# Retention states of the sample tokens read before they are decayed, and three smaller moves around it

## The chip, the cores and the metric

The kernel runs on one core of one Trainium2 chip. The time is the device time of one execution in microseconds (us), the median of several. A core has a matrix engine (TensorE, PE; PEld is its load of the stationary operand), a vector engine (VectorE, DVE), ScalarE (ACT), GpSimd (POOL), SyncE (SP, which here only issues transfers), and 16 DMA engines that move data between its on-chip memory and HBM.

## What is computed

One layer of a decoder for two groups that share the weights: 256 prompt tokens and 8 sample tokens (264 columns in all), width 1024, float32. What the change touches:

```
mkv = rmsnorm(mem_prompt, norm_mem) @ w_mem_kv          # memory keys and values, 256 rows
mk, mv = jnp.split(mkv, 2, axis=-1)                      # both are also outputs
# retention, per head (4 heads, DK = 256, DV = 512); for a sample token the chunk is one token long
att = einsum('bhnk,bhmk->bhnm', qc, kc) * dmask
o = einsum('bhnm,bhmv->bhnv', att, vc) + einsum('bhnk,bhkv->bhnv', qc * q_decay[..., None], s)
s = s * s_decay + einsum('bhmk,bhmv->bhkv', kc * k_decay[..., None], vc)
o = o * lax.rsqrt(mean(o * o, axis=-1) + EPS)
```

For a sample token the query meets the state as it comes in: o = (q.k) v + gamma (q @ s), and the state that goes out is gamma s + k v. That is equal to q @ (gamma s + k v). Behind the mixers, which are projected and merged, comes a mixture of 32 experts whose weights (192 MB) are streamed once.

## The kernel before

Activations lie transposed, 8 tiles of 128 channels by 264 tokens. `tensor_order` (L274) writes out one list of tasks for the whole kernel up to the router, and PE, ACT and DVE each walk that list and do their part of a task, in order, with semaphores between them. A projection task (`ux`, `q`, `ga`, `lru_out`, ...) gives one tile of 128 output channels: 8 float32 products of 128x128 by 264 columns (`project`, L940), which the profile counts as 16 matmul records. Two tasks share a weight chunk of 1 MB. SP loads chunks into a ring of five; chunk n is issued once the last task on chunk n-5 is done on PE. Results go to PSUM, four banks in turn for projections and three for the rest (bank 7 is apart), and ACT or DVE empties a bank before its next use. `weave(main, side)` spreads one list evenly over another.

**Start.** SP issues the memory rows `memT` in two halves, the constants, chunk 0, `xT` and the next chunks. ACT squares the memory rows, PE sums the squares over channels with 8 products by a matrix of ones (`column_sums`, L959), ACT takes the root, DVE the reciprocal and then norms eight tiles (L1548); `mk` (L990) starts on these. `mk` gives keys as rows (token by channel), and four `mkT` tasks (L1013, 4 transposes each) turn them. The squares of `x` go the same way (`x_sq`, 8 products).

**States.** There are 16 sample states of 1 MB, each two heads of one sample (task number s), in three buffers `st`. POOL issues the load (L853) and, after the update, the store (L878). The row of v that a state needs is first moved to partition 0 (L859) and then spread over the partitions (L863, `partition_broadcast`). Task `sd` decays a state in place on ACT (L1268, 2 instructions) and adds k v on DVE (L1701, 4 instructions); task `so` on PE (L1136) multiplies the updated state by the query of its sample, into bank 7, at row group 32h for head h. In POOL's loop, each turn is: wait for the update of s, store s, move the row for s+2 and wait for it, broadcast, load s+2. The `sd` of the next state stands ahead of `so` in the list, on ACT and DVE too. Around them run the 32 projections `ga`, `lru_out`, `gc`, `mem_out`, and the prompt's retention: `att` (scores of a head, L1111 and L1114, masked by DVE into the one buffer `attT`, L1691) and four `o` per head (L1124).

**After the states.** `soT` turns the samples' result (L1144, 4 transposes), then per head ACT squares (`oq`), PE sums (`on`, 4 products, L959) and DVE norms. `gb`, `g`, `ret_out` and `x2` projections follow, then the router. SP issues the first expert weights when `ret_ready` has counted all 16 tiles of the gated retention (after the last `g`); from some 750 us on the experts run behind the stream of weights (L770).

## Time and profile before

| | us |
|---|---|
| median of 3 runs (1208.28 to 1210.97) | 1209.36 |
| the profiled execution, its own time | 1210.15 |
| its span | 1208.3 |
| PE busy | 988.2 (82%) |
| DVE busy | 361.3 (30%) |
| ACT busy | 225.6 (19%) |
| POOL busy | 99.4 (8%) |
| DMA, mean over the span | 285 GB/s |

The profile is of one execution. Busy time is by engine; what counts is who waits for whom in each stretch. The stretches are: memory keys and values up to about 77 us, projections and gates to 317 us, the states to about 510 us, the rest of the mixers to 700 us, the router to 766 us, the experts to 1192 us.

### The profile page before, as it was taken

How to read it: one execution, taken by the hardware profiler on the slowest of the kernel's cores; microseconds unless marked ns; L12 is line 12 of the kernel's file. 1: busy time of each engine (PE TensorE's matmuls, PEld its weight loads, DVE VectorE, ACT ScalarE, POOL GpSimd, SP SyncE). 2: the span in 40 equal slices, each digit the busy share in tenths (PEclk: the TensorE clock that was granted, in tenths of full speed). 3: DMA queues.
4: the chain of work that ended last, by engine and by line, in shares of the span. 5: the costliest groups of instructions: out<-in, count | busy, mean ns of one | idle time of the engine just before them, and what ended most of it. 6: DMA issues, size and time to landing. Idle time of an engine off the chain costs nothing.

```text
span 1208.3 us, 16378 instructions
## 1 busy us (share of the span) xinstructions
PE 988.2 (82%) x7006; PEld 716.5 (59%) x7006; DVE 361.3 (30%) x660; ACT 225.6 (19%) x465; POOL 99.4 (8%) x122
## 2 busy tenths in 40 slices
PE   6999999999998899799999978666666665665654
PEld 5888888778775566488888835433333333333323
DVE  1201583376223334323211172111135111111113
ACT  2211213204412221142100051101010101010102
POOL 0001111000123233100000050000000000000000
PEclk9999999999999899899999999999987889899888
DMA  9764557494667787643534958999999999999991
GB/s 289 242 233 161 175 178 274 162 294 114 216 224 248 272 290 248 236 139 120 194 106 139 383 208 339 417 417 416 417 416 416 416 416 417 417 417 417 417 411 69
DMA packets 138826, 343.80 MB, mean 285 GB/s; under 512 B 7640, under 2 KB 91864, under 8 KB 122360
## 3 DMA queue, kind: packets, MB, share of 16 engines
q1 hardware_dynamic: 124288, 290.04, 63.7%
q0 software_dynamic: 14464, 52.68, 12.3%
q8 instruction: 58, 0.95, 0.3%
q14 instruction: 16, 0.13, 0.0%
HBM read 320.46 MB, written 22.20 MB: 284 GB/s over the span
## 4 chain that ended last, share of the span: by engine, by line
PE 46%; SPq 24%; DMA 11%; issue 7%; DVE 7%; ACT 3%; POOL 2%; DVEq 0%; ACTq 0%; POOLq 0%
PE psum L940 27%; SPq L770 24%; DMA arena<-in_w_up 6%; PE psum L990 5%; DMA arena<-in_state_ret 4%; PE psum L949 2%; PE psum L682 2%; ACT arena L1268 2%; DVE arena L1701 2%; DMA arena<-arena 1%; PE psum L692 1%; PE psum L959 1%; POOL arena L863 1%; PE psum L666 1%; DVE arena L1600 1%
## 5 line engine op out<-in xcount | busy, mean ns | idle before, releaser
L940 PE MATMUL psum<-arena 128*128 128x264 f32 x2048 | 473.1, 388 | 0.0
L940 PEld LDWEIGHTS psum<-arena 128*128 128x128 f32 x2048 | 386.3, 190 | 83.9 <-issue 20.0
L682 PE MATMUL psum<-arena 128*32 128x256 f32 x2048 | 148.1, 440 | 119.4 <-DMA arena<-in_w_up 118.7
L682 PEld LDWEIGHTS psum<-arena 128*32 128x32 f32 x2048 | 79.0, 123 | 183.1 <-issue 160.5
L1268 ACT ACTIVATE arena<-psum 128x264 f32<-128x264 f32 (+4 forms) x180 | 75.1, 434 | 322.8 <-PE psum L940 251.9
L1268 ACT ACTIVATE arena<-arena 128x1024 f32<-128x1024 f32 (+7 forms) x67 | 58.7, 903 | 202.6 <-DMA arena<-in_state_ret 106.6
L1701 DVE SCALAR_TENSOR_TENSOR arena<-arena 128x512 f32<-128x512 f32 x64 | 52.9, 888 | 121.7 <-ACT arena L1268 107.1
L1887 DVE SCALAR_TENSOR_TENSOR arena<-arena,psum 128x128 f32<-128x128 f32 x32 | 9.2, 288 | 238.4 <-ACT arena L1476 238.4
L692 PE MATMUL psum<-arena 128*32 128x256 f32 x1024 | 65.2, 397 | 11.7 <-ACT arena L1488 11.7
L1196 PE MATMUL psum<-arena 128*128 128x264 f32 x112 | 39.8, 438 | 25.9 <-DVE arena L1899 25.9
L990 PE MATMUL psum<-arena 128*128 128x256 f32 x256 | 56.3, 379 | 3.1 <-DVE arena L1548 3.1
L692 PEld LDWEIGHTS psum<-arena 128*32 128x32 f32 x1024 | 31.0, 113 | 39.7 <-ACT arena L1488 21.6
L990 PEld LDWEIGHTS psum<-arena 128*128 128x128 f32 x256 | 48.2, 190 | 9.8 <-issue 3.4
L1476 ACT ACTIVATE arena<-psum 128x128 f32<-128x128 f32 x32 | 8.9, 278 | 241.2 <-PE psum L682 241.2
L1136 PE MATMUL psum<-arena 128*8 128x512 f32 x128 | 36.4, 698 | 20.6 <-DVE arena L1701 20.6
L666 PEld LDWEIGHTS psum<-arena 128*128 128x128 bf16 x576 | 35.4, 104 | 16.9 <-issue 16.9
L666 PE MATMUL psum<-arena 128*128 128x128 bf16 x576 | 40.5, 230 | 1.6 <-DVE arena L1835 1.6
L1196 PEld LDWEIGHTS psum<-arena 128*128 128x128 f32 x112 | 17.2, 194 | 39.9 <-DVE arena L1899 37.5
L1842 DVE COPY arena<-psum 32x256 f32<-32x256 f32 x32 | 13.5, 421 | 75.7 <-PE psum L692 75.7
L1899 DVE TENSOR_TENSOR arena<-arena,psum 128x264 f32<-128x264 f32 x56 | 24.0, 428 | 38.7 <-PE psum L1196 38.7
L863 POOL PARTITION_BROADCAST arena<-arena x16 | 22.2, 1389 | 117.9 <-DMA arena<-arena 117.9
L949 PE MATMUL psum<-arena 128*128 128x264 f32 x128 | 29.8, 386 | 0.0
(236 smaller groups left out, 696.3 us busy)
## 6 DMA issues: line engine op xcount, KB each, us to landing
arena<-in_w_gate SPq DMA_DIRECT2D x64, 1024.0 KB, 23.0
arena<-in_w_up SPq DMA_DIRECT2D x64, 1024.0 KB, 22.5
arena<-in_w_down SPq DMA_DIRECT2D x64, 1024.0 KB, 22.9
arena<-in_w_in SPq DMA_DIRECT2D x48, 1024.0 KB, 5.2
arena<-in_state_ret POOLq DMA_DIRECT2D x16, 1024.0 KB, 6.5
out_ret_s<-arena POOLq DMA_DIRECT2D x16, 1024.0 KB, 7.9
arena<-in_w_mem_kv SPq DMA_DIRECT2D x8, 1024.0 KB, 9.6
arena<-in_cache_mem_k POOLq DMA_DIRECT2D x8, 1024.0 KB, 5.7
```

Source lines behind the costliest of these rows:

```text
L666: mm = pe.matmul(psum[:, 5 + k // 4, (k % 4) * P:(k % 4 + 1) * P], xr[x][:, t, k * P:(k + 1) * P], Sb[:, t, :], start=t == 0 and x == 0, s ...
L682: mm = pe.matmul(psum[32 * a:32 * a + SLOTS, bank, 0:256], tokens[:, 4 * half + k, SLOTS * j:SLOTS * (j + 1)], w[:, :, k, P * a:P * (a + 1 ...
L692: mm = pe.matmul(psum[32 * a:32 * a + SLOTS, bank, 0:256], hidden[:, SLOTS * (2 * half + f):SLOTS * (2 * half + f + 1)], w[:, f, 256 * a:2 ...
L770: sp.dma_start(into(s, i), expert_part(e, i)).then_inc(chunk_loaded[s], 16)
L863: nc.gpsimd.partition_broadcast(vb[:, s % 2, :], v_row0[0:1, :], P).then_inc(v_bcast, 1)
L940: mm = pe.matmul(ps(task)[:, 0:T], w[:, k, (i % 2) * P:(i % 2 + 1) * P], rhs[:, k, :], start=k == 0, stop=k == KT - 1 and not two)
L949: mm = pe.matmul(ps(task)[:, 0:T], w[:, k, (i % 2) * P:(i % 2 + 1) * P], rhs[:, KT + k, :], start=False, stop=k == KT - 1)
L990: mm = pe.matmul(ps(task)[:, 0:256], memT[:, k, m * P:(m + 1) * P], w[:, k, :], start=k == 0, stop=k == KT - 1)
L1136: mm = pe.matmul(psum[32 * h:32 * h + NS, 7, :], QM[:, 2 * h + i, b, :], st[:, s % 3, 2 * h2 + i, :], start=b == 0 and i == 0, stop=b == N ...
L1196: pe.matmul(psum[:, 7, 0:T], yS[:, (q - 1) % 2, d * P:(d + 1) * P], SwT[:, (q - 1) % 2, :], start=True, stop=True).then_inc(scatter_full, 1)
L1268: steps.did(nc.scalar.activation(out, in_, func, **kw), sem)
L1701: did(V.scalar_tensor_tensor(x, vb[:, s % 2, h2 * DV:(h2 + 1) * DV], kT[:, 2 * (2 * hp + h2) + i, TP + b:TP + b + 1], x, ALU.mult, ALU.add ...
```

## The change

1. **Start.** `chan` (channel constants) is issued first, chunk 0 between the halves of `memT`. DVE scales the memory rows by `norm_mem` alone (`memS`), and `mk` and `mv` run on these. The factor of a row (one over its root mean square) is applied as results leave PSUM: for `mk`, which is now computed already transposed (weights stationary), by DVE; for `mv` by ACT, with a column that the new task `mrow` makes. `mkT` is gone. The output `mem_k` is stored from the transposed tile.
2. **Squares.** DVE adds the tiles of squares pairwise (`add_squares`), and `column_sums` is one product. It holds for `mem_sq`, `x_sq` and the four `on`.
3. **States.** `so` waits for the load of its state, not for the update, and stands ahead of `sd`; ACT's decay waits for `so`. Its four products go to four column groups (one per tile of the state, 16 columns each) instead of two. `soT` multiplies by a table `place`, which adds the two halves of a head and applies gamma; (q.k) v is made apart (tasks `qk`, and four DVE products at `vs`). The row of v is moved two states ahead into one of two buffers, and the load of s+2 is issued before the store of s.
4. **Scores.** `att` of the next head stands a head ahead, `attT` has two buffers.

The diff, cut to its core:

```diff
@@ tensor_order
-    ret = []
+    ret = [("att", 0)]
     for h in heads:
-        ret += [("att", h)] + [("o", h, j) for j in range(4)]
-    so = [("sd", 0)]
-    for s in range(2 * NS):
-        so += ([("sd", s + 1)] if s + 1 < 2 * NS else []) + [("so", s)]
+        ret += ([("att", h + 1)] if h + 1 < HEADS else []) + [("o", h, j) for j in range(4)]
+    so = [x for s in range(2 * NS) for x in (("so", s), ("sd", s))]
+    middle = weave(branches, ret[1:])
...
-        [("mem_sq",)] + t("mk", 8)[:2] + [("xq",)] + t("mk", 8)[2:4] + [("x_sq",), ("lam",)] + t("mk", 8)[4:]
-        + weave(t("mv", 8), t("mkT", 4)) + t("mq", 8) + t("mqs", 2)
+        t("mk", 8)[:2] + [("mem_sq",), ("xq",)] + t("mk", 8)[2:4] + [("mrow",)] + t("mk", 8)[4:6]
+        + [("x_sq",), ("lam",)] + t("mk", 8)[6:] + t("mv", 8) + t("mq", 8) + t("mqs", 2)
...
-        + weave(weave(branches, ret[1:]), so)
+        + middle[:4] + weave(middle[4:], so)
@@ gpsimd
+            def v_row(s):
+                b, hp = n_state(s)
+                if s >= 2:
+                    pool.wait_ge(v_bcast, s - 1)
+                pool.dma_start(v_row0[:, s % 2, :], vs_rows[b:b + 1, hp * D:(hp + 1) * D]).then_inc(v_row_in[s % 2], 16)
             def v_broadcast(s):
-                b, hp = n_state(s)
-                if s >= 1:
-                    pool.wait_ge(v_bcast, s)
-                pool.dma_start(v_row0[0:1, :], vs_rows[b:b + 1, hp * D:(hp + 1) * D]).then_inc(v_row_in, 16)
-                pool.wait_ge(v_row_in, 16 * (s + 1))
+                pool.wait_ge(v_row_in[s % 2], 16 * (s // 2 + 1))
                 if s >= 2:
                     pool.wait_ge(st_updated, s - 1)
...
+                if s + 2 < 2 * NS:
+                    v_row(s + 2)
...
             for s in range(2 * NS):
+                if s >= 1 and s + 2 < 2 * NS:
+                    load_state(s + 2)
                 pool.wait_ge(st_updated, s + 1)
                 pool.dma_start(dst, st[:, s % 3]).then_inc(st_out[s % 3], 16)
                 if s + 2 < 2 * NS:
                     v_broadcast(s + 2)
-                    if s >= 1:
-                        load_state(s + 2)
@@ tensor
+            def column_sums(task, src, cols, n):
+                pe.wait_ge(squares_added, n)
+                begin(task)
+                end(task, pe.matmul(ps(task)[:, 0:cols], ones, src[:, 0, 0:cols], start=True, stop=True))
...
+                        mm = pe.matmul(ps(task)[:, 0:TP], w[:, k, (i % 2) * P:(i % 2 + 1) * P], memS[:, k, :],
+                                       start=k == 0, stop=k == KT - 1)
...
                 elif kind == "so":
-                    pe.wait_ge(st_updated, s + 1)
-                    for i in range(2):
-                        for h2 in range(2):
-                            h = 2 * hp + h2
-                            mm = pe.matmul(psum[32 * h:32 * h + NS, 7, :], QM[:, 2 * h + i, b, :],
-                                           st[:, s % 3, 2 * h2 + i, :],
-                                           start=b == 0 and i == 0, stop=b == NS - 1 and i == 1)
+                    pe.wait_ge(q_placed, 2)
+                    pe.wait_ge(st_in[s % 3], 16 * (s // 3 + 1))
+                    for g in range(4):
+                        mm = pe.matmul(psum[32 * g:32 * g + 2 * NS, 7, :], QM[:, 4 * hp + g, b, :], st[:, s % 3, g, :],
+                                       start=s == 0, stop=s == 2 * NS - 1)
                     mm.then_inc(st_read, 1)
@@ scalar
                     act.wait_ge(st_in[s % 3], 16 * (s // 3 + 1))
+                    act.wait_ge(st_read, s + 1)
@@ vector
+            for q in range(2):
+                dve.wait_ge(mem_in[q], 16)
+                did(V.tensor_tensor(memS[:, 4 * q:4 * q + 4, :], memT[:, 4 * q:4 * q + 4, :],
+                                    bc(cvs("norm_mem")[:, 4 * q:4 * q + 4].unsqueeze(2), (P, 4, TP)), ALU.mult), mem_scaled)
...
+            def take_mem_keys(i):
+                full(dve, ("mk", i))
+                v(V.tensor_tensor(mkT[:, i, :], ps(("mk", i))[:, 0:TP], rstd[:, 0, 0:TP], ALU.mult), free_of(("mk", i)))
```

The order of PE's instructions at the start, before. L959 is the sum of squares, L990 `mk` and then `mv`, L1013 `mkT`:

```order
L959 MATMUL psum<-arena 128x256 x8
L990 MATMUL psum<-arena 128x256 x32
L959 MATMUL psum<-arena 128x264 x8
L990 MATMUL psum<-arena 128x256 x40
L1013 MATMUL psum<-arena 128x128 x4
```

And now, where L1015 is `mk`, L1027 `mv`, L978 a sum of squares, L1002 `mrow`:

```order
L1015 MATMUL psum<-arena 128x256 x16
L978 MATMUL psum<-arena 128x256
L1015 MATMUL psum<-arena 128x256 x16
L1002 MATMUL psum<-arena 128x8 x2
L1015 MATMUL psum<-arena 128x256 x16
L978 MATMUL psum<-arena 128x264
L1015 MATMUL psum<-arena 128x256 x16
L1027 MATMUL psum<-arena 128x256 x64
```

Two tasks of `mk` stand ahead of the first sum, each sum is one product, and no transposes stand between the projections.

POOL's queue in the loop over the states, before, with what each waits for. L859 moves the row of v, L863 (ISA) broadcasts it, L853 loads a state, L878 stores one:

```order
L859 DMA arena<-arena 1x16x64 [waits v_bcast]
L863 ISA arena<-arena 128x1024 [waits st_updated,v_row_in]
L853 DMA arena<-in_state_ret 128x4x512 [waits st_read,st_out_0]
L878 DMA out_ret_s<-arena 128x4x512 [waits st_updated]
L859 DMA arena<-arena 1x16x64 [waits v_bcast]
```

And now, with L873 for the row, L880 for the broadcast, L866 for the load and L901 for the store:

```order
L880 ISA arena<-arena 128x1024 [waits st_updated,v_row_in_0]
L873 DMA arena<-arena 1x16x64 [waits v_bcast]
L866 DMA arena<-in_state_ret 128x4x512 [waits st_read,st_out_0]
L901 DMA out_ret_s<-arena 128x4x512 [waits st_updated]
L880 ISA arena<-arena 128x1024 [waits st_updated,v_row_in_1]
```

The row is now issued behind the broadcast, for a state two further on; the load is held only by the store of the state that had its buffer, and no broadcast stands between that store's landing and the load.

PE at the start of the states, before. L940 is a projection, L1111 and L1114 `att`, L1124 and L1125 `o`, L1136 `so`:

```order
L1111 MATMUL psum<-arena 128x256 x2
L1114 MATMUL psum<-arena 128x128 x2
L940 MATMUL psum<-arena 128x264 x8
L1124 MATMUL psum<-arena 128x256
L1125 MATMUL psum<-arena 128x128
L940 MATMUL psum<-arena 128x264 x8
L1124 MATMUL psum<-arena 128x256
L1125 MATMUL psum<-arena 128x128
L1136 MATMUL psum<-arena 8x512 x4
```

And now, L961 a projection, L1139 and L1142 `att`, L1152 and L1153 `o`, L1164 `so`:

```order
L1139 MATMUL psum<-arena 128x256 x2
L1142 MATMUL psum<-arena 128x128 x2
L961 MATMUL psum<-arena 128x264 x8
L1139 MATMUL psum<-arena 128x256 x2
L1142 MATMUL psum<-arena 128x128 x2
L961 MATMUL psum<-arena 128x264 x8
L1152 MATMUL psum<-arena 128x256
L1153 MATMUL psum<-arena 128x128
L961 MATMUL psum<-arena 128x264 x8
L1164 MATMUL psum<-arena 16x512 x4
```

The second `att` comes before the first `o`, and the first `so` one projection later; the number of products of `so` is the same, with 16 stationary columns instead of 8.

## Rows read from the trace of the kernel before

**Rows 1.** Busy time by stretch: PE, weight loads, DVE, ACT, POOL, granted clock, DMA

```profile
core 0: us, PE busy (x) PEld busy (x) DVE busy (x) ACT busy (x) POOL busy (x), PEclk, DMA share, GB/s
...
168.00:317.00 149.00, 148.74 (x778) 120.32 (x777) 79.81 (x58) 41.23 (x84) 15.83 (x20) 1.00 0.64 205
345.00:510.00 165.00, 145.04 (x623) 98.83 (x621) 55.72 (x78) 34.15 (x51) 43.38 (x52) 0.95 0.77 264
...
766.00:1192.00 426.00, 265.13 (x3274) 149.52 (x3262) 88.58 (x230) 48.33 (x132) 0.00 (x0) 0.90 0.99 405
```

**Rows 2.** PE in order of time, first 60 us: start, duration, instructions

```profile
7.29 5.71 PE L959 MATMUL psum<-arena 128*128 128x256 f32 x16 [7.29 <-ACT arena L1268]
...
16.07 14.05 PE L990 MATMUL psum<-arena 128*128 128x256 f32 x64 [3.07 <-DVE arena L1548]
...
29.96 3.72 PE L959 MATMUL psum<-arena 128*128 128x264 f32 x16
...
50.79 0.60 PE L1013 MATMUL psum<-arena 128*128 128x128 f32 x4
```

**Rows 3.** DMA issues at 0.7, 2.8 and 4.4 us: KB each, us to landing

```profile
arena<-in_memT SPq DMA_DIRECT2D x1, 512.0 KB, 4.0
...
arena<-in_w_mem_kv SPq DMA_DIRECT2D x1, 1024.0 KB, 7.4
...
arena<-in_w_mem_kv SPq DMA_DIRECT2D x1, 1024.0 KB, 11.8
```

**Rows 4.** Who waited for whom, 317 to 515 us: total, times, longest

```profile
POOL arena L863 <- DMA arena<-arena: 117.9, 16, 10.4
...
PE psum L1136 <- DVE arena L1701: 20.6, 6, 5.9
...
PE psum L1124 <- DVE arena L1691: 2.4, 2, 1.6
```

**Rows 5.** PE in order of time, state stretch; in brackets idle time before

```profile
320.37 1.10 PE L1111 MATMUL psum<-arena 128*128 128x256 f32 x4
...
352.95 1.89 PE L1136 MATMUL psum<-arena 128*8 128x512 f32 x8
...
366.78 3.36 PE L1136 MATMUL psum<-arena 128*8 128x512 f32 x8 [3.31 <-DVE arena L1701]
...
506.63 3.41 PE L1136 MATMUL psum<-arena 128*8 128x512 f32 x8 [2.40 <-DVE arena L1701]
```

**Rows 6.** The chain of waits in the same stretch: start, duration

```profile
372.83 2.01 ACT arena L1268 x2
...
375.63 3.01 DVE arena L1701 x3
```

**Rows 7.** DMA queues (packets, MB, share) and issues, 317 to 515 us

```profile
q0 software_dynamic: 9216, 33.62, 48.1%
q1 hardware_dynamic: 16153, 16.28, 25.4%
...
arena<-in_state_ret POOLq DMA_DIRECT2D x16, 1024.0 KB, 6.5
out_ret_s<-arena POOLq DMA_DIRECT2D x16, 1024.0 KB, 7.9
```

**Rows 8.** The stores of the states, line L878, all sixteen

```profile
DMA to landing us min/median/max: 4.7/7.9/11.4
```

**Rows 9.** Line L878 from 350 to 370 us: stores right behind a load

```profile
L878 POOL DMA_DIRECT2D out_ret_s<-arena x2: 759/773/787, 353.3 to 367.0; - x2
...
DMA to landing us min/median/max: 8.3/9.8/11.2
```

**Rows 10.** The chain of waits in the expert stage, one line

```profile
748.95 3.45 PE psum L682 x64
```

**Rows 11.** PE in order of time, behind the states: one `on`

```profile
524.76 1.94 PE L959 MATMUL psum<-arena 128*128 128x264 f32 x8
```

**Rows 12.** SyncE's issues: the first load of an expert's weights

```profile
664.32 0.46 SPq L755 DMA_DIRECT2D arena<-in_w_gate  x1
```

More of the change, by code:

```diff
@@ L121 @@
     "memT": (KT * TP, "load", "mem"),
+    "memS": (KT * TP, "load", "mem"),
+    "mrow": (8, "load", "mem"),
     "sq": (KT * T, "load", "mem"),
@@ L951, in project @@
                 end(task, mm)
-            def column_sums(task, src, n, cols, first=None):
+            def column_sums(task, src, cols, n):
+                pe.wait_ge(squares_added, n)
                 begin(task)
-                for k in range(n):
-                    if first is not None and k % 4 == 0:
-                        pe.wait_ge(squares, first + k // 4)
-                    mm = pe.matmul(ps(task)[:, 0:cols], ones, src[:, k, 0:cols], start=k == 0, stop=k == n - 1)
-                end(task, mm)
+                end(task, pe.matmul(ps(task)[:, 0:cols], ones, src[:, 0, 0:cols], start=True, stop=True))
             def residual_squares(k):
@@ L1023, in _ @@
                     _, h, l = task
-                    read(pe, ("mkT", 3))
+                    read(pe, last["mk"])
                     read(pe, last["mq"])
```

184 lines of the change are left out of this document (119 added, 65 removed).

## The prediction

> **What bounds the kernel now.** I read busy time by stretch first. From 168 to 317 us PE is busy 148.7 of 149 us: a microsecond of PE work less there is a microsecond off the time. From 766 to 1192 us the DMA share is 0.99, and no engine sets the pace: the stream of expert weights takes its length whenever it starts [rows 1]. SyncE issues its first load at 664.3 us [rows 12], behind the last `g` on PE. So the end moves with PE's arrival there, and the question is how much earlier PE arrives. The stretch ahead of it in which PE is not full is 345 to 510 us, with 145.0 of 165 us busy at a granted clock of 0.95 [rows 1].
>
> Next, who waits there: PE for DVE's state update ahead of `so`, 20.6 us in six waits, and 2.4 us for the masked scores [rows 4]. Behind them POOL waits 117.9 us, sixteen times, for the one row of v, because that 4 KB transfer is queued behind a 1 MB store and often a load, and the next load is issued only after it. After some waits `so` also runs slower: 3.36 us behind an idle 3.31 us, 1.89 us at 352.95 with no wait [rows 5], which is the lower of the two clock levels (1.2 GHz) against the higher (2.4 GHz). A wait so costs a little more than itself.
>
> **Start.** PE's first `mk` begins at 16.1 us, after squares summed from 7.3 us, root, reciprocal and norm [rows 2]. Now it needs only DVE's scaled rows and chunk 0. The first chunk landed at 2.8 + 7.4 = 10.2 us, the second at 4.4 + 11.8 = 16.2 us [rows 3], with `xT` (1056 KB) and itself between: 6.0 us for 2 MB, 3.0 us per MB. Some 0.7 MB that stood ahead of chunk 0 now stand behind it, so it lands at about 8.0 us and the second half of `memT` at 9.5. DVE's scaling of a half I put at 1.2 us (four tiles; the first `mk` waits for the second half at 10.7 us). `mk` 0 ends at about 13 and `mk` 1 at 16.5 us, where two took (16.07, 14.05 for four) until 23.1: 6.6 us gained. Chunk 1 lands at 16.2, just in time. Each sum of squares shrinks from 16 records (3.72 us, [rows 2]) to 2, say 0.45: for `x_sq` 3.2 us gained; the memory's own, formerly under the start, now costs 0.45, and `mrow` 0.5. The four `mkT` (0.60 us of records each, [rows 2], some 0.43 in the flow) give 1.7 us. DVE's pairwise adds (1.8 records of a 1056-column pass, about 2 us) and evacuations lie beside `mk` work; if DVE were late the fifth `mk` would wait for its bank, but it has 6 us. Sum 6.6 + 3.2 + 1.7 - 1.0 = 10.5; I take **10**, from 7 (chunk 1 late by 3 us) to 11.
>
> The small task `qk` adds two products, 0.5 us.
>
> **States, PE's own work.** The stretch from the first `att` (320.4) to the first `gb` (510.0 + 3.6 = 513.6: `so` 15 ends at 510.0 [rows 5], and `mem_out` 7 follows) is 193.2 us. Take away the waits, 23.0 us [rows 4], and the slow clock behind four of them (1.5 us each, 3.36 against 1.89 [rows 5]) and one slow projection, 7 us. What is left is 163. `so` costs 1.89 us for 8 records of 512 columns in two column groups. Over four groups the expert stage gives the price: 64 records of 256 columns in 3.45 us [rows 10], 0.054 each, so 8 of twice the columns 0.86 us, with a switch 0.95. Sixteen times 0.94 less is 15: PE's floor for the stretch is **148**, with `so` 15 at 143 and one `so` each 8.9 us.
>
> **States, the other chain.** Once PE no longer waits for the update, a buffer comes free only when its store has landed, and POOL waits for exactly that ahead of the next load. A turn of its loop is then: wake 0.3, issue a load 0.8, issue the store, its landing L. So the period is P = L + 1.1 us, and PE waits for it wherever P is above 8.9. The first `so` comes about 14.3 us after `att` (two `att`, three projections, one `o`); then 0.95, decay 2.0, update 3.7 (four instructions; three take 3.0) [rows 6], and gaps give the first store at 22. The load for state 15 is issued 13 P - 0.8 later and lands 6.5 us after [rows 7]: `so` 15 starts at 27.6 + 13 P. What is L? All sixteen stores land in 4.7, median 7.9, at most 11.4 us [rows 8]. But the changed loop issues each store right behind a load; two such cases took 8.3 and 11.2 [rows 9], and the 11.4 is another: mean 10.3. I take the middle of 7.9 and 10.3, **9.1**, since the row's wait, which made POOL late and the pairs tight, is gone. P is 10.2, `so` 15 at 160.2, and `gb` 0 5.3 us later (`so`, one `o`, one projection) at 165.5 instead of 193.2: **27.7** gained. The waits of some 1.3 us each are shorter than those behind which the clock had fallen. DMA agrees that it is close: 33.6 MB of states took 48.1% of 198 us, 3.0 us per MB, and 16.3 MB of weights 25.4%, 3.2 us per chunk [rows 7]; a period moves two and one, 9.2 us of 16 engines.
>
> The masked scores a head ahead take the 2.4 us, already in. The row of v, two ahead, hides behind a period.
>
> **A page on this.** The Trainium skill (DMA: Bandwidth & Descriptors, Queues, rings and completion order) says that each DMA engine takes turns between the queues that have work, packet by packet. This speaks against the change: a pair of load and store shares with a weight chunk whenever SP has one. By that rule the tight pairs' 11.2 and 8.3 us are one with a chunk beside it and one without, and with a chunk each time the sum would be that of the slow loop below, 1183 or more. The same page (Anatomy of one DMA) fits a transfer as 2.0 us plus bytes at 436 GB/s, by which I estimate 4.4 us for a state; with that the loop would never hold PE, and the sum would be 1151 us. The fastest store here took 4.7 us and the median 7.9, so the trace decides for the longer.
>
> **Behind the states.** Four `on` of 8 records (1.94 us, less 0.16 of overlap, [rows 11]) become 2 records each: 5.3 us gained. `soT` goes from 4 transposes to 8 short records with full weight loads, 0.8 us lost. DVE's two adds per head and ACT's first square, which waits for the last store (now some 11 us after `so` 15, as the update comes behind it), lie under `gb` tasks of 3.6 us. Sum **4.5**.
>
> **Sum.** 10 - 0.5 + 27.7 + 4.5 = 41.7. Against the profiled execution (1210.15) that is 1168.5; it stands 0.8 above the median of the runs, so 1167.7. I say **1168 us**.
>
> **Rivals.**
> - *PE's floor.* Stores land in 7.8 us or less, the loop hides, and `gb` 0 comes at 148.7: 44.5 in place of 27.7, 1151 us. For it: the median landing of 7.9 (P 9.0), and no broadcast between. Against: DMA has 9.2 us of work in 8.9. Chance 0.30.
> - *The loop is slow.* Load, store and chunk share all the way: L of 10.3 gives P 11.4, `so` 15 at 175.8, 15.6 us worse: 1183. At L 11.4 (the longest) 1198. For it: the tight pairs. Chance 0.20, some 0.05 of it above 1192.
> - *The change does not free PE.* `so` reads a raw state, yet the wait just changes its name from update to load, at the old pace. `so` 15 would come 186 us after the first `att`, as now (506.6 - 320.4 [rows 5]), and only the 14 us of start, `qk` and end are gained, with 1.7 of a shorter tail: 1193.5. That is a period of 12.2, and its chance is in the 0.05 just named.
> - *Slower.* The mechanism is the same loop, in order on POOL: a late store holds the next load, and with it the store behind it. The total is 1209.35 - 14 - (193.2 - 32.9 - 13 P), which crosses 1209.3 at P = 13.4, a store landing of 12.3 us. At P = 14 it gives 1217. Speaking for it: DMA would be asked for more in less time than before. Against: no store of the sixteen took over 11.4 [rows 8]. Chance 0.05.
> - Within 0.2%: only by chance between the last two, 0.02.
>
> **How the numbers follow.** The forecast, P between 9.6 and 10.9 and so 1160 to 1177 us, has 0.43. Low 1148 is PE's floor with 3 us more from the start; high 1192 leaves out the end of the slow loop, no gain and slower, about 0.12, and below 1148 I leave 0.04. A measurement of this kernel tells 0.2% (2.4 us) from no change. Faster by more 0.93, within 0.02, slower 0.05.
>
> **What would show it.** `mk` begins near 9 us with a short wait for the second half, and `x_sq` is one product. `so` takes 0.95 us. PE's waits for a DVE update are gone and waits of 1 to 3 us for the state's DMA stand in their place, in the later half, some 15 us in all; stores land in about 9 us. From the first `gb` to the first expert load everything is as before but 4.5 us shorter, and the expert stretch keeps its 426 us. The forecast is wrong if `so` waits for nothing (first rival), if stores take over 10 us, or if the start shows a wait for chunk 1.

## The result, and the profile of the changed kernel

The changed kernel takes 1172.63 us (median of four runs, 1167.83 to 1174.22), the kernel before 1208.82 (median of four, 1201.39 to 1210.97). The ratio is 0.9705, with a 95% interval of 0.9654 to 0.9755. The forecast was 1168, with a range of 1148 to 1192. The profiled execution took 1173.44 us with a span of 1171.6 us, where that of before had 1208.3: 36.7 us less. Three places in the trace divide this sum into four parts, and each has its forecast:

| part of the span | before | after | gained | forecast |
|---|---|---|---|---|
| to the first `att` | 320.4 | 311.15 | 9.2 | 9.5 |
| first `att` to first `gb` | 193.2 | 172.0 | 21.2 | 27.7 |
| first `gb` to the first expert load | 150.7 | 145.8 | 4.9 | 4.5 |
| first expert load to the end | 544.0 | 542.7 | 1.3 | 0 |

The start first: four separate lines from PE's and DVE's order of time, 0 to 75 us. The bracket gives the idle time just before and what ended it.

```profile
8.63 8.80 PE L1015 MATMUL psum<-arena 128*128 128x256 f32 x32 [8.63 <-DMA arena<-in_w_mem_kv]
...
10.06 1.23 DVE L1578 TENSOR_TENSOR arena<-arena 128x1024 f32<-128x1024 f32 x1 [3.51 <-DMA arena<-in_memT]
...
17.26 0.59 PE L978 MATMUL psum<-arena 128*128 128x256 f32 x2
...
31.96 0.61 PE L978 MATMUL psum<-arena 128*128 128x264 f32 x2
```

PE begins `mk` at 8.63 us where it began at 16.07 [rows 2]. Chunk 0 is what it waited for, and it came 0.6 us behind the time of the working (8.0 us). The scaling of the second half takes 1.23 us, as taken, and both sums are two records instead of sixteen. The two tasks end at 17.4 us, a microsecond later than worked out. No wait for chunk 1 follows: the one wait of PE up to 80 us is that of 8.6 us for chunk 0.

Next the stretch that mattered: busy time by stretch, with the columns of [rows 1], first the stretch of the states, then the expert stage.

```profile
311.00:483.00 172.00, 154.43 (x739) 116.77 (x737) 55.48 (x88) 44.01 (x68) 50.52 (x59) 0.97 0.85 281
...
729.00:1155.00 426.00, 268.15 (x3286) 150.52 (x3278) 88.91 (x232) 48.09 (x132) 0.00 (x0) 0.90 0.99 405
```

PE is busy 154 of 172 us, so it is still not the bound there. The expert stage is 426 us at a share of 0.99, as before [rows 1]. Who waited for whom, 300 to 495 us (total, times, longest), the view of [rows 4]:

```profile
POOL arena L866 <- DMA out_ret_s<-arena: 82.4, 13, 8.5
...
POOL out_ret_s L901 <- DVE arena L1772: 25.2, 3, 11.6
...
PE psum L1164 <- DMA arena<-in_state_ret: 17.4, 11, 3.0
...
POOL arena L880 <- DMA arena<-arena: 8.3, 1, 8.3
```

Read it from the top. POOL's 117.9 us of waits for the row of v [rows 4] have shrunk to one of 8.3 us, and in their place POOL waits 82.4 us, thirteen times, for a store to land before it may issue a load (L866). PE's 20.6 us of waits for DVE's update are gone, and 17.4 us of waits for a state's load stand there: in all, PE waits only 5.6 us less than before (17.4 against 23.0). One turn of POOL's loop and the start of the next, in order of time, show its period:

```profile
405.20 0.79 POOL L866 DMA_DIRECT2D arena<-in_state_ret  x1 [5.60 <-DMA out_ret_s<-arena]
405.98 0.76 POOL L901 DMA_DIRECT2D out_ret_s<-arena  x1
406.76 1.29 POOL L880 PARTITION_BROADCAST arena<-arena  x1
...
415.48 0.78 POOL L866 DMA_DIRECT2D arena<-in_state_ret  x1 [6.61 <-DMA out_ret_s<-arena]
416.26 0.76 POOL L901 DMA_DIRECT2D out_ret_s<-arena  x1
```

Load and store are issued 0.8 us apart, and the next load comes as soon as that store has landed: 10.28 us from L866 to L866. The thirteen loads of the loop (340.61 to 467.83 us) are 10.6 us apart in the mean. The landings in this stretch, the view of [rows 7], with the median in the last column:

```profile
arena<-in_state_ret POOLq DMA_DIRECT2D x16, 1024.0 KB, 7.1
out_ret_s<-arena POOLq DMA_DIRECT2D x16, 1024.0 KB, 9.3
```

Last, PE in order of time, as [rows 5] shows it for before:

```profile
325.27 1.05 PE L1164 MATMUL psum<-arena 128*16 128x512 f32 x8
...
369.37 1.05 PE L1164 MATMUL psum<-arena 128*16 128x512 f32 x8 [1.95 <-DMA arena<-in_state_ret]
370.35 1.22 PE L1152 MATMUL psum<-arena 128*128 128x256 f32 x2
...
392.89 1.05 PE L1164 MATMUL psum<-arena 128*16 128x512 f32 x8 [3.03 <-DMA arena<-in_state_ret]
...
394.96 5.07 PE L961 MATMUL psum<-arena 128*128 128x264 f32 x16
...
476.19 1.91 PE L1164 MATMUL psum<-arena 128*16 128x512 f32 x8 [2.61 <-DMA arena<-in_state_ret]
...
479.47 7.36 PE L961 MATMUL psum<-arena 128*128 128x264 f32 x32
```

`so` takes 1.05 us in four column groups, where it took 1.89 in two [rows 5]. The last `so` begins 165.0 us after the first `att` (476.19 - 311.15); before it was 186.3, and the forecast 160.2.

### The profile page after: what moved, and what is told of

It is laid out like the page before. It is cut to its first block, busy times and chain, and to the rows that moved or that the text cites. A ratio compares the mean times of both kernels' runs of the same rounds, so it can differ in the third digit from the quotient of the medians.

```text
span 1171.6 us, 16329 instructions
## 1 busy us (share of the span) xinstructions
PE 961.7 (82%) x6950; PEld 705.9 (60%) x6950; DVE 366.6 (31%) x681; ACT 221.4 (19%) x453; POOL 100.9 (9%) x122
## 4 chain that ended last, share of the span: by engine, by line
PE 47%; SPq 22%; DMA 20%; DVE 5%; issue 4%; ACT 2%; POOL 1%; DVEq 0%; ACTq 0%; POOLq 0%
PE psum L961 28%; SPq L783 22%; DMA out_ret_s<-arena 10%; DMA arena<-in_w_up 8%; PE psum L693 3%; PE psum L1015 3%; PE psum L970 2%; PE psum L1027 2%; PE psum L703 2%; PE psum L677 1%; ACT arena L1301 1%; DVE arena L1664 1%; DMA arena<-arena 1%; POOL arena L866 1%; DMA arena<-in_state_ret 1%
## 5 line engine op out<-in xcount | busy, mean ns | idle before, releaser
L961 PE MATMUL psum<-arena 128*128 128x264 f32 x2048 | 473.6, 388 | 0.0
L961 PEld LDWEIGHTS psum<-arena 128*128 128x128 f32 x2048 | 387.6, 191 | 76.3 <-issue 12.0
L1301 ACT ACTIVATE arena<-psum 128x264 f32<-128x264 f32 (+5 forms) x160 | 67.5, 439 | 350.8 <-PE psum L961 269.0
L703 PE MATMUL psum<-arena 128*32 128x256 f32 x1024 | 66.4, 402 | 11.8 <-ACT arena L1522 11.7
L1772 DVE SCALAR_TENSOR_TENSOR arena<-arena 128x512 f32<-128x512 f32 x64 | 45.6, 774 | 82.0 <-ACT arena L1301 81.9
L1229 PEld LDWEIGHTS psum<-arena 128*128 128x128 f32 x112 | 17.1, 193 | 38.6 <-DVE arena L1977 36.1
L1015 PE MATMUL psum<-arena 128*128 128x256 f32 x128 | 30.1, 396 | 8.6 <-DMA arena<-in_w_mem_kv 8.6
L1301 ACT ACTIVATE arena<-psum,arena 128x256 f32<-128x256 f32 (+2 forms) x49 | 22.8, 473 | 72.1 <-PE psum L1027 24.9
L1977 DVE TENSOR_TENSOR arena<-arena,psum 128x264 f32<-128x264 f32 x56 | 24.0, 428 | 36.7 <-PE psum L1229 36.7
L1015 PEld LDWEIGHTS psum<-arena 128*128 128x128 f32 x128 | 25.4, 200 | 12.3 <-issue 8.6
L1164 PE MATMUL psum<-arena 128*16 128x512 f32 x128 | 17.7, 624 | 17.6 <-DMA arena<-in_state_ret 17.4
```

Of the source, the lines that this page charges most:

```text
L703: mm = pe.matmul(psum[32 * a:32 * a + SLOTS, bank, 0:256], hidden[:, SLOTS * (2 * half + f):SLOTS * (2 * half + f + 1)], w[:, f, 256 * a:2 ...
L961: mm = pe.matmul(ps(task)[:, 0:T], w[:, k, (i % 2) * P:(i % 2 + 1) * P], rhs[:, k, :], start=k == 0, stop=k == KT - 1 and not two)
L1015: mm = pe.matmul(ps(task)[:, 0:TP], w[:, k, (i % 2) * P:(i % 2 + 1) * P], memS[:, k, :], start=k == 0, stop=k == KT - 1)
L1229: pe.matmul(psum[:, 7, 0:T], yS[:, (q - 1) % 2, d * P:(d + 1) * P], SwT[:, (q - 1) % 2, :], start=True, stop=True).then_inc(scatter_full, 1)
L1301: steps.did(nc.scalar.activation(out, in_, func, **kw), sem)
L1772: did(V.scalar_tensor_tensor(x, vb[:, s % 2, h2 * DV:(h2 + 1) * DV], kT[:, 2 * (2 * hp + h2) + i, TP + b:TP + b + 1], x, ALU.mult, ALU.add ...
```

## The experiments

Two theories stood against each other. **A** is the prediction's: with the wait for the update gone, POOL's loop (a load waits for the store before it) sets the pace, P = L + 1.1. **B** is its rival: the DMA engines are simply full (share 0.85 in this stretch), and the order on POOL matters little. The part-by-part experiments are made on the changed kernel, one on the kernel before. "Stretch" is first `att` to first `gb` in the run's own profile, of one execution each. Times of one kernel differ between executions: the four of the changed kernel span 6.4 us, four of another kernel below 9.9 us. Where only one execution was timed, a difference of a few microseconds is not told from none.

### Store ahead of the load

```diff
-                if s >= 1 and s + 2 < 2 * NS:
-                    load_state(s + 2)
                 pool.wait_ge(st_updated, s + 1)
                 pool.dma_start(dst, st[:, s % 3]).then_inc(st_out[s % 3], 16)
                 if s + 2 < 2 * NS:
                     v_broadcast(s + 2)
+                    if s >= 1:
+                        load_state(s + 2)
```

> The changed kernel with one move: POOL issues the store of state s and the broadcast ahead of the load of s+2, not behind it. The stretch from the first att to the first gb was 193.2 us before the change and 172.0 us with it, against a floor of PE work of 148. Theory A (POOL's order): a store that is ready stands behind a load that waits for the previous store to land, so the period is a landing plus 1.1 us; freed of that, the period falls to 8.9 to 9.3 us and the stretch to 150 to 157 us, the time to about 1155 us. Theory B (the DMA engines are simply full, share 0.85 in this stretch): the period stays at 10.3 to 10.6 us, the stretch at 168 to 172 us and the time at 1169 to 1173 us.

Measured: 1179.2 us (1175.2 to 1180.5) against 1206.3 for the kernel before on the same chip, ratio 0.9783 (0.975 to 0.9815); stretch 172.8. Theory A asked for a stretch of 150 to 157 us and missed. The stretch is just above B's 168 to 172, but the rows show another cause than B's. POOL in order of time, two stores and the load between, then its and PE's waits, 311 to 484 us:

```profile
411.05 0.75 POOL L899 DMA_DIRECT2D out_ret_s<-arena  x1 [9.35 <-DVE arena L1772]
...
413.95 0.79 POOL L866 DMA_DIRECT2D arena<-in_state_ret  x1
...
421.12 0.75 POOL L899 DMA_DIRECT2D out_ret_s<-arena  x1 [6.39 <-DVE arena L1772]
```

```profile
POOL out_ret_s L899 <- DVE arena L1772: 97.2, 14, 11.5
...
PE psum L1164 <- DMA arena<-in_state_ret: 18.8, 9, 5.4
```

No store is waited for by POOL any more (the sixteen land in a median of 5.8 us here). POOL now waits 97.2 us for DVE's *update*, and the load stands behind it in POOL's queue. The update in turn can start only behind `so`, which reads the raw state and needs its load. Four rows show that chain between the load at 413.95 and the load of s + 4 at 433.45:

```profile
420.29 1.05 PE L1164 MATMUL psum<-arena 128*16 128x512 f32 x8 [0.43 <-DMA arena<-in_state_ret]
...
425.13 0.39 ACT L1301 ACTIVATE arena<-psum 128x264 f32<-128x264 f32 x1 [4.86 <-PE psum L961]
425.42 1.99 ACT L1301 ACTIVATE arena<-arena 128x1024 f32<-128x1024 f32 x2
...
427.51 2.74 DVE L1772 SCALAR_TENSOR_TENSOR arena<-arena 128x512 f32<-128x512 f32 x4 [6.69 <-ACT arena L1301]
```

The load lands 6.2 us after its issue, `so` of s + 2 takes 1 us, the decay starts 4.1 us behind it, decay and update take 4.8, and 3 us later the load of s + 4 is issued: 19.5 us for two periods. The 4.1 us are no work on the state. `weave` has put a projection between `so` and `sd`, and ACT, in order, empties that projection's bank first (the row at 425.13). So POOL's queue in order, the raw read and this place in ACT's list hold the loop together. No run moves the decay right behind `so`.

### Reading the raw state with the old loop

```diff
+                v_row(s)
                 pool.wait_ge(v_row_in[s % 2], 16 * (s // 2 + 1))
...
-                if s + 2 < 2 * NS:
-                    v_row(s + 2)
```

(and the load behind the broadcast, as above, and no rows moved ahead of the loop)

> The changed kernel with POOL's loop as it was before: the row of v for s+2 is moved behind the store of s and waited for, then broadcast, then the load. so still reads the raw state. If the row's wait was what made the loop slow, the stretch from the first att to the first gb returns to 183 to 193 us (time 1184 to 1194). If the raw read is what frees PE, it stays near 172 us (time near 1173).

Measured: 1218.66 us, one execution; stretch 217.1, beyond the 183 to 193 expected for the row's wait, the last `so` 209.5 us after the first `att`. That is slower than the kernel before (1206.3 on this chip), in spite of the start, `on` and the column groups. Of the waits, 320 to 545 us:

```profile
POOL arena L881 <- DMA arena<-arena: 95.5, 16, 9.2
...
PE psum L1161 <- DMA arena<-in_state_ret: 54.8, 8, 10.5
```

POOL waits again sixteen times for the 4 KB row behind a big store, and PE pays 54.8 us. In the kernel before, the decay ran ahead of PE's `so` and hid part of that; a raw read puts `so`, decay and update in series behind each load. That reading is argued; what is shown is that with POOL's old loop the raw read, and the smaller moves beside it, come with a stretch 24 us longer than before. So the raw read does not make the gain.

### The decayed and updated state read, in the changed loop

```diff
-    so = [x for s in range(2 * NS) for x in (("so", s), ("sd", s))]
+    so = [("sd", 0)]
+    for s in range(2 * NS):
+        so += ([("sd", s + 1)] if s + 1 < 2 * NS else []) + [("so", s)]
...
-                    pe.wait_ge(st_in[s % 3], 16 * (s // 3 + 1))
+                    pe.wait_ge(st_updated, s + 1)
...
-                    act.wait_ge(st_read, s + 1)
```

> The changed kernel with so behind the update again, as before the change (the order of sd and so too), and the new POOL loop kept; the samples' result then counts the decay and k v twice, the work is the same. Theory A (POOL's loop with its store landings sets the pace): the period stays at 10.5 us and each so comes one decay and update later, 5 to 7 us, so the stretch is 177 to 181 us and the time about 1180. Theory C (the raw read is the gain): the stretch returns to 188 to 193 us, the time to 1189 to 1194.

Measured: 1178.83 us, one execution; stretch 177.8, the last `so` 170.4 us after the first `att`, 5 us later than in the changed kernel. Both are A's numbers (177 to 181, about 1180): the pace is the loop's, whichever form of the state PE reads. The raw read is worth some 6 us with this loop.

### A quarter of each store

```diff
-                pool.dma_start(dst, st[:, s % 3]).then_inc(st_out[s % 3], 16)
+                pool.dma_start(dst[:, 0:1], st[:, s % 3, 0:1]).then_inc(st_out[s % 3], 16)
```

> The changed kernel, but only a quarter of each state is stored (the rest of the output is left out), so a store moves 256 KB. If the waits of so for its load (17.4 us in eleven) come from stores that land late, the landing falls to 5 us or less, the waits go and the stretch is PE's floor of 148 to 151 us, the time 1149 to 1153. If something else holds PE there (evacuation by ACT or DVE, the decay and update), the stretch stays above 160 us.

Measured: 1157.05 us, one execution; stretch 152.9, the last `so` 147.6 us after the first `att`. The stores' landings and PE's waits, 311 to 530 us:

```profile
out_ret_s<-arena POOLq DMA_DIRECT2D x16, 256.0 KB, 5.4
...
PE psum L1164 <- DMA arena<-in_state_ret: 4.1, 2, 3.0
```

With stores landing in 5.4 us PE waits twice, and the stretch is 5 us above the floor of 148 that the prediction worked out. Stretch, time and landing are each a little above what was expected (148 to 151, 1149 to 1153, 5 or less). Both halves of A stand all the same: L holds the loop, and PE's own work below it is 148.8 (152.9 less 4.1 of waits). It does not tell whether what counts is the landing time or the bytes; the last experiments do.

### The store issued by ACT

```diff
+            def store_state(s):
+                b, hp = n_state(s)
+                act.wait_ge(st_updated, s + 1)
+                act.dma_start(dst, st[:, s % 3]).then_inc(st_out[s % 3], 16)
...
+                    if s >= 1:
+                        store_state(s - 1)
                     act.wait_ge(st_in[s % 3], 16 * (s // 3 + 1))
```

(and POOL stores nothing; ACT stores the last state at `soT`)

> The changed kernel with the stores of the states issued by ACT, each ahead of the next state's decay, and no store in POOL's queue. POOL then issues the load of s+2 when the store of s-1 has landed and nothing else waits behind it. Both POOL orders tried so far gave a period of 10.3 to 10.6 us: with the load first a ready store waits for a landing (82 us of such waits), with the store first a load waits for the update (97 us). Theory A (the coupling of loads and stores in one queue that is issued in order): the period falls to 8.9 to 9.4 us, the stretch from the first att to the first gb from 172 to 149 to 158 us, and the time to 1152 to 1161 us. Theory B (the DMA engines' throughput holds it at 10.3 us): 168 to 173 us and a time near 1172. Theory C (ACT becomes the bound, since it now waits for updates and empties banks late): 173 to 185 us.

Measured: 1185.96 us (1183.41 to 1189.73) against 1207.4, ratio 0.9862 (0.9785 to 0.9938); stretch 183.2. A had asked for a gain and failed here; 183.2 is in the range of theory C (173 to 185), in which ACT becomes the bound. The waits, 311 to 500 us:

```profile
POOL arena L866 <- DMA out_ret_s<-arena: 101.1, 12, 14.6
...
PE psum L1161 <- DMA arena<-in_state_ret: 26.6, 7, 7.2
```

ACT reaches the store only ahead of the next decay, and that is a period behind the update. The store lands faster (7.9 us) but starts later, and POOL waits 14.6 us for it at worst. C had named late emptying of banks by ACT as well; PE has no wait for it here. The second queue gained nothing, since the engine that feeds it comes by too seldom.

### Two column groups, scores behind, squares and the sum in their old places

Four kernels, one execution each, that undo one edit of the change. Two column groups in `so`:

```diff
-                    for g in range(4):
-                        mm = pe.matmul(psum[32 * g:32 * g + 2 * NS, 7, :], ...)
+                    for g in (0, 2, 1, 3):
+                        at = 32 * (g // 2)
+                        mm = pe.matmul(psum[at:at + 2 * NS, 7, :], ...)
```

(and `place` adds the two halves accordingly)

> The changed kernel with so's four products in two column groups, as before the change. Each so takes 1.85 to 1.9 us instead of 1.05. If the loop over the loads sets the pace from the fifth state on, most of it lies under the waits (17.4 us in eleven): the stretch grows from 172 by 2 to 5 us and the time to about 1176. If PE's work sets it, by 13 to 14 us, to 1186.

Measured: 1171.36 us, stretch 169.7, `so` 1.90 us. Sixteen times 0.85 us more on PE, and nothing lost, where 2 to 5 us were expected: it disappears in PE's waits for the loads, which are 7.1 us here instead of 17.4.

The scores of a head right ahead of its `o`:

```diff
-    ret = [("att", 0)]
+    ret = []
     for h in heads:
-        ret += ([("att", h + 1)] if h + 1 < HEADS else []) + [("o", h, j) for j in range(4)]
+        ret += [("att", h)] + [("o", h, j) for j in range(4)]
```

(and one buffer for `attT`)

> The changed kernel with each att directly ahead of its own head's o, and one buffer for the masked scores, as before the change. Before, PE waited 2.4 us in two places for it. If the loop over the states swallows it, the time stays within 3 us of 1172.6; otherwise it grows by 2 to 5 us.

Measured: 1173.96 us, stretch 171.0. No difference that one execution can tell.

All squares summed by PE, without DVE's adds:

```diff
-                end(task, pe.matmul(ps(task)[:, 0:cols], ones, src[:, 0, 0:cols], start=True, stop=True))
+                for k in range(tiles_):
+                    mm = pe.matmul(ps(task)[:, 0:cols], ones, src[:, k, 0:cols], start=k == 0, stop=k == tiles_ - 1)
+                end(task, mm)
```

> The changed kernel with the squares summed by PE as before (8 products for the memory and for x, 4 for each of four heads), nothing added on DVE. By the prediction's prices: 3.1 us for each of the first two and 5.3 for the four, 11.5 us, so about 1184. If PE's work is hidden in these places, less.

Measured: 1181.12 us. The first `att` comes at 317.6 instead of 311.15, 6.45 us later, and the part behind the states is 5.3 us longer; the stretch between is 166.5, 5.5 us shorter. So undoing the edit costs 8.5 us of the total (1184 was expected). In the two parts where PE is full it costs 11.8, and the loop gives some of that back.

The memory's sum ahead of the first `mk`, as before:

```diff
-        t("mk", 8)[:2] + [("mem_sq",), ("xq",)] + t("mk", 8)[2:4] + ...
+        [("mem_sq",)] + t("mk", 8)[:2] + [("xq",)] + t("mk", 8)[2:4] + ...
```

(and DVE's scaling behind the reciprocal)

> The changed kernel with the sum of the memory's squares ahead of mk again, and the scaled rows made only after its root and reciprocal (result the same). It takes out the early start alone. By the prediction PE's first mk comes near 17 to 18 us instead of 8.6 with a hold to 11, so the time grows by 6 to 8 us, to about 1180. If chunk 1 or a later chunk held mk anyway, it grows by less than 4.

Measured: 1182.18 us; the first `att` at 321.7, 10.6 us later, where 6 to 8 was expected. PE in order of time:

```profile
13.67 1.19 PE L978 MATMUL psum<-arena 128*128 128x256 f32 x2 [13.67 <-DVE arena L1581]
...
18.64 16.69 PE L1015 MATMUL psum<-arena 128*128 128x256 f32 x64 [3.77 <-DVE arena L1598]
```

DVE's adds end only at 13.67 us, later than PE's own sum over raw squares would (it began at 7.29 [rows 2]). Pre-added squares need the memory product ahead of them; put first, they leave PE idle for longer.

### The updated state read, and the store first

The first three experiments leave two couplings: with the raw read the update is late, with the load first the store must land. So I took both away: PE reads the updated state (and no `qk` product), and POOL issues the store, then the load. The result is whole. It is the two diffs above together, with the decay factor 1.0 in the placement table and the correction for `qk` left out:

```diff
-                place[32 * (2 * (h % 2) + i) + NS * (h // 2) + b, NS * h + b] = 1.0 - 2.0 ** (-5.0 - h)
+                place[32 * (2 * (h % 2) + i) + NS * (h // 2) + b, NS * h + b] = 1.0
```

> The changed kernel with so reading the updated state again (place holds 1 instead of gamma, and qk and its products are gone, so the result is whole), and with the store and the broadcast ahead of the load in POOL's queue. Everything else of the change stays. Theory A (a cycle of waits through the update): with the raw read the update starts only behind so, and with the store first the next load is issued behind that update, 10.3 us per state. Here decay and update start as the load lands: from one update to the load of s+2 3.2 us, its landing 6.8, decay 2.0 and update 3.7, 16 us for two states, so a period of 8 and PE's 8.9 decides. The stretch from the first att to the first gb falls from 172 to 149 to 156 us, the time to 1149 to 1158. Theory B (the DMA engines' throughput is the bound at 10.3 us however the waits lie): 168 to 175 us, the time 1169 to 1176.

Measured: **1152.39 us** (1151.96 to 1152.99) against 1206.3, ratio 0.956 (0.9528 to 0.9592); stretch 150.5. Its interval lies wholly below that of the changed kernel's ratio (0.9654 to 0.9755), so it beats both kernels. PE in order of time, then busy time of 155 us and of the middle of them, and PE's only waits for a state (two):

```profile
331.30 1.05 PE L1166 MATMUL psum<-arena 128*16 128x512 f32 x8 [1.13 <-DVE arena L1766]
...
340.25 1.05 PE L1166 MATMUL psum<-arena 128*16 128x512 f32 x8
...
349.20 1.05 PE L1166 MATMUL psum<-arena 128*16 128x512 f32 x8
```

```profile
325.00:480.00 155.00, 153.13 (x757) 117.28 (x756) 61.76 (x98) 50.03 (x72) 46.71 (x55) 1.00 0.88 309
...
340.00:450.00 110.00, 110.00 (x549) 82.85 (x548) 43.39 (x71) 33.89 (x50) 38.93 (x46) 1.00 0.99 347
```

```profile
PE psum L1166 <- DVE arena L1766: 1.9, 2, 1.1
```

One `so` each 8.95 us, PE busy 153.1 of 155 us with a granted clock of 1.00 throughout. The same states and weight chunks pass in less time than in the changed kernel: 309 GB/s at a share of 0.88 here, 281 at 0.85 there. Bytes and DMA engines were not what held that kernel, so B falls. But they are near their end in this one: from 340 to 450 us the share is 0.99, beside a PE that is busy throughout, and loads now land in a median of 9.3 us, stores in 7.5. The loop's period, for which 8 us had been counted with a landing of 6.8, is by this some 8.6 (by my estimate 3.2 + 9.3 + 2.0 + 2.7 us for two states), little less than PE's 8.95. How much a kernel with less PE work would still gain is not shown.

The same with two column groups in `so`:

> The kernel of e_updated_store_first (1152.4 us, no wait of PE left in the stretch) with so's four products in two column groups. Under the waits of the changed kernel two groups cost nothing (1171.4 against 1172.6). Where PE's own work is the bound, the 0.85 us more of each so must all count: 13 to 14 us, the time 1165 to 1167. If the period of the loop (8 us by my count) or the DMA engines lie right under PE's 8.9, it is the same, since they only get more room; less than 10 us would mean that PE is not the bound there.

Its edit is the one shown above for `so`. Measured: 1166.0 us, one execution, 13.6 above; stretch 163.3, 12.8 above. Sixteen times 0.85 is 13.6: what was hidden in the changed kernel counts in full where PE is the bound.

| stretch, us | load first | store first |
|---|---|---|
| raw state read | 172.0 | 172.8 |
| updated state read | 177.8 | 150.5 |

Neither change alone gains anything (0.8 and 5.8 us longer), and both together gain 21.5.

### The row of v ahead, on the kernel before

```diff
+            def v_row(s):
...
+                if s >= 2:
+                    pool.wait_ge(v_bcast, s - 1)
+                pool.dma_start(v_row0[:, s % 2, :], vs_rows[...]).then_inc(v_row_in[s % 2], 16)
...
             def v_broadcast(s):
...
-                pool.dma_start(v_row0[0:1, :], vs_rows[...]).then_inc(v_row_in, 16)
-                pool.wait_ge(v_row_in, 16 * (s + 1))
+                pool.wait_ge(v_row_in[s % 2], 16 * (s // 2 + 1))
...
+                if s + 2 < 2 * NS:
+                    v_row(s + 2)
```

> The kernel before with one part of the change: the row of v is moved two states ahead into one of two buffers, and not waited for behind the store. The order of store, broadcast and load, the read of the updated state, two column groups, the start and the squares are as before. If the row's wait was what made the loop slow, PE's waits (23.0 us) and the slow clock behind them (7 us) go and the stretch from the first att to the first gb falls from 193.2 to 163 to 168 us, the time by 25 to 30 us to 1178 to 1184. If the raw read or the four groups are needed for it, the time stays above 1195.

Measured: 1187.38 us (1180.85 to 1190.79) against 1203.67, ratio 0.9812 (0.9732 to 0.9893). Expected were 1178 to 1184 and a stretch of 163 to 168, so both missed: the gain is real, since the interval lies below 1, but it is 16 us between the medians where 25 to 30 were expected. Its profiled execution is the slowest of the four. Stretch 168.4, the last `so` 163.0 us after the first `att`. Outside the stretch that execution is 5.5 us longer than the one of before, 3.3 of it ahead of the first `att`; the granted clock of its first 20 us was 0.88, against 1.00. PE's one wait for a state, 320 to 495 us:

```profile
PE psum L1140 <- DVE arena L1705: 3.7, 1, 3.7
```

This single edit takes 24.8 us out of the stretch, and the change as a whole 21.2. These are two executions, and 3.6 us between them may be chance. But everything else that the change does between the first `att` and the first `gb` (raw read, loads as buffers come free, four column groups, scores ahead) shows no further gain. This kernel has the loop of the fastest one, which reads the updated state and stores first; what the fastest has more in this stretch is the four column groups and the scores ahead.

## Why the prediction was right, and where not

**Start: right.** 9.2 us where 9.5 were forecast. Chunk 0, scaling and `mk` stand within a microsecond of their places. By e_sum_first and e_squares_on_pe the two halves of this gain (the product ahead, 10.6, and the adds, 6.45) overlap; without the product ahead the first `att` comes at 321.7, later than in the kernel before (320.4).

**Behind the states: right.** 4.9 us where 4.5 were forecast; undoing the adds gave 5.3 back.

**The form P = L + 1.1: right.** The twelve stores issued behind a load, from 352 us on, landed in 8.2 to 11.1 us, 9.6 in the mean, so P should be 10.7; the loads are 10.6 us apart and the last ten `so` 10.7. A quarter of each store freed PE, as the form says. L had been taken as the middle of two numbers, 7.9 and 10.3, and that 9.1 fell so near is in part luck.

**The stretch: mis-sized by 6.5 us.** The forecast put the last `so` at 160.2 after `att`, and it came at 165.0. The terms of that sum, against the rows: the first store came at 24.4 (335.58 - 311.15) instead of 22, since the decay stands 4.1 us behind `so`, after a projection (326.3 to 330.4 us); the twelve periods from the load of state 3 to that of state 15 had 10.6 instead of 10.2, 5 us; the first store landed in 4.7 us instead of L, which gave 4.4 back; and the last load took 8.4 us from issue to `so` instead of 6.5. The rest, 1.7 us, comes from the start of the last `so` on and is the clock: `so` took 1.91 us behind an idle 2.61 instead of 1.05, and `o` 1.22 instead of 0.59. I had excluded slow records behind waits, on the ground that the waits would be shorter than those behind which the clock had fallen before. The rows say otherwise: behind 1.95 us idle two records took 1.22 instead of 0.59, and behind 3.03 us a projection took 5.07 instead of 3.73. By comparing such turns with undisturbed ones I estimate some 5 us in all; but where POOL's loop sets the pace, slow records ahead of the last `so` only shorten the next wait. PE's waits themselves were forecast as some 15 us and measured 17.4. The end gave 1.3 us more and the part behind 0.4 more than forecast, so the total missed by less: 36.7 of 41.7.

**The cause: half wrong.** "Once PE no longer waits for the update" took the raw read for what frees PE, and "the row's wait, which made POOL late, is gone" stood as a side remark. The runs turn this round. The row moved ahead takes 24.8 us out of the stretch by itself on the kernel before. The raw read lengthens the chain through a buffer (load, `so`, decay, update, store), and with the old loop the kernel is slower than before. The step that failed is the pricing of the three edits (raw read, row ahead, load ahead of the store) as one. The sum came out because the loop that they make together is the one that I costed; as an account of what brings the gain it was luck.

**Column groups: right in size, wrong in place.** The 15 us off PE's floor are real (13.6 measured, where PE sets the pace) and are nothing in the changed kernel. The prediction gave the floor as 148 and the loop as 165.5, so this follows from it, but it never said that this edit was then worth nothing (stretch 169.7 without it, 172.0 with it). On PE the 21.2 us gained are some 14 us less work and 5.6 us less waiting, the rest the clock; without the groups PE works that much longer and waits that much less.

**"DMA agrees that it is close": right in sense, not as a price.** I took 3.0 us of 16 engines as the cost of a state of 1024 KB. The same transfers measured 3.2 in the changed kernel and 2.8 in the fastest (57.4% and 52.8% of 155 us, for 29.0 and 30.5 MB), so the number is no constant, and 9.2 us of work in a period of 8.9 was too much: the fastest kernel passes all of it in 8.95. But the share there is 0.99 in the middle of the stretch, so DMA was close indeed. The objection to the first rival, "9.2 us of work in 8.9", failed by these few per cent.

**The page's rule.** Stores issued right behind a load, with a chunk in most periods, landed in a median of 9.3 us, where the fastest store of before took 4.7 [rows 8]. The Trainium skill (DMA: Bandwidth & Descriptors, Queues, rings and completion order) has each DMA engine take turns between queues. That speaks of the chunk alone, since load and store are both in POOL's queue (q0 of [rows 7]). The long landings are in keeping with it, but no run here takes the chunk away. The slow loop that I derived from it, an L above 10, did not come. The same page's fit (Anatomy of one DMA), by my estimate 4.4 us for a state, is met by no median in company; e_store_first, at 5.8, comes nearest.

**Rivals.** PE's floor (1151) did not come, since stores took over 7.8 us; it is what e_updated_store_first reached by another way (1152.4). "Does not free PE" had its mechanism half right, for the wait did change its name, 20.6 us for the update to 17.4 for the load; but the pace was 10.6 us and not 12.2. "Slower" is refuted by the landings, though e_row_behind shows that the raw read with one more link in POOL's queue gives it.

**Open.** How the landings of load and store divide between the queues was not taken apart: a store took 9.3 us right behind a load, and issued ahead of one 5.8 us in e_store_first and 7.5 in the fastest kernel; each order changes the neighbours too. Why the stretch gets 3 to 5 us shorter when it starts later (e_sum_first, e_squares_on_pe) is not settled; SyncE's chunks fall otherwise against the states there, but no run holds them fixed. The price of the raw read for the fastest kernel (raw, with the load issued by a third engine) was not tried, nor was the decay right behind `so`, 4 us earlier, which the chain of e_store_first asks for.

## What to carry to other kernels

An engine that issues loads, stores and small moves in order turns each wait ahead of one into a wait of the next. So write the whole cycle of a buffer (load, read, update, store, load again) as one chain through that queue and count its turns, before making any single read earlier. A saving on an engine that waits elsewhere is worth nothing until that wait goes and everything afterwards: price it in both cases. And where a change has several edits that are costed together, the edit that carries the gain is known only when each is undone or done alone. Last, a task that is ready may still stand behind another in its engine's list: look for such places before calling a chain the length of its work.

## What the runs showed of the hardware

- A DMA share is no price of bytes. From 325 to 480 us, 1024 KB of state traffic took 3.0 us of 16 engines in the kernel before (258 GB/s), 3.2 in the changed kernel (282) and 2.8 in the fastest (309). At a share of 0.99 the fastest moved 347 GB/s, and the expert stage 405.
- In the changed kernel, where stores of 1 MB are issued 0.8 us behind a load, they landed in a median of 9.3 us and the loads in 7.1. Issued 3 us ahead of the load, they landed in 5.8 us in one kernel (e_store_first) and in 7.5 in a faster one (e_updated_store_first), where the loads took 9.
- In the kernel before, POOL waited up to 10.4 us for a move of 4 KB inside the chip that was issued behind a store of 1 MB [rows 4].
- Eight records of 512 columns took 1.05 us in four column groups and 1.89 to 1.90 in two; the rows of a switch between these and full products show no gap above 0.1 us.
- In the changed kernel the three waits of PE of 1.95, 2.61 and 3.03 us were followed by records at the lower of the two clock levels, and those of 1.2 to 1.74 us were not. A wait of 2.67 us in e_store_first and one of 3.02 us in the kernel before were not either.
